# Two transformer blocks on one core: key scores searched in on-chip memory while queries are formed, a new order of the side work, and an earlier handover to the down weights

## The reference, cut to what matters

```
q = (ht @ peer_wq).reshape(T, 8, 256)                      # T = 512 tokens, 8 heads
s1 = einsum("thd,hnd->thn", q[..., :128], k1)              # 128 keys per half
s2 = einsum("thd,hnd->thn", q[..., 128:], k2)
v1, i1 = top_k(s1, 16);  v2, i2 = top_k(s2, 16)
cand = v1[..., :, None] + v2[..., None, :]                 # 16 x 16 pairs
sc, pos = top_k(cand, 16)
experts = i1[pos // 16] * 128 + i2[pos % 16]               # 128 of 16384 a token
gates = softmax(sc)
a = gelu(peer_u[experts] . h) * gates
out = sum over the 128 experts of a * peer_v[experts]
```

## Time and profile before

| | |
|---|---|
| median of 3 runs | 3027.76 us (3025.11 to 3029.04) |
| the profiled execution's own time | 3026.6 us |
| its span, first to last instruction | 3024.8 us |
| mean granted TensorE clock | 0.973 |
| busy share of the span: PE, DVE, ACT, POOL | 94%, 74%, 49%, 20% |
| moved between memory and chip | 746.30 MB, 247 GB/s on average |

### The profile page before, as it was taken

The page is one execution under the profiler, slowest core; times in us unless marked ns, Lnnn a source line. Parts: engine busy times, 40 slices in busy tenths (PEclk is TensorE's granted clock), DMA queues, the critical chain, the costliest instruction groups (busy, mean ns, idle before and its releaser), DMA issues.

```text
span 3024.8 us, 37310 instructions
## 1 busy us (share of the span) xinstructions
PE 2845.1 (94%) x13639; PEld 2369.9 (78%) x13639; DVE 2236.1 (74%) x3019; ACT 1481.4 (49%) x1990; POOL 598.8 (20%) x480
## 2 busy tenths in 40 slices
PE   5979987999999989999999998898999999999998
PEld 3657756888888758776777788898999987888887
DVE  6465547888888853797954329999997867888886
ACT  3443235878888733544452432564665633333332
POOL 0200111111111100000000010033234434444442
PEclk7999988999999999999999998999999999999999
DMA  7544535999999833232333334587789999999995
GB/s 300 169 159 157 198 132 219 362 371 366 362 354 356 305 130 114 96 119 84 105 132 132 129 119 157 180 306 264 273 303 361 337 373 341 365 367 360 362 362 187
DMA packets 203628, 746.30 MB, mean 247 GB/s; under 512 B 24752, under 2 KB 78128, under 8 KB 146352
## 3 DMA queue, kind: packets, MB, share of 16 engines
q1 hardware_dynamic: 124656, 497.12, 45.8%
q0 software_dynamic: 56912, 179.26, 16.9%
q10 hardware_dynamic: 21872, 67.48, 5.8%
HBM read 670.80 MB, written 98.11 MB: 254 GB/s over the span
## 4 chain that ended last, share of the span: by engine, by line
PE 56%; DVE 18%; issue 5%; ACT 3%; DMA 3%; ACTq 0%; DVEq 0%; POOL 0%; SPq 0%; POOLq 0%
PE PS L550 48%; DVE wlo L1897 3%; DVE oh L2673 2%; DVE hf L2687 2%; DVE hf L2699 1%; PE PS L1151 1%; ACT whi L1227 1%; PE PS L1017 1%; PE PS L1029 1%; PE PS L856 1%; ACT HH L1867 1%; DVE zo L2422 1%; DVE sS L2726 1%; DVE i L2569 1%; DVE wkk L2572 1%
## 5 line engine op out<-in xcount | busy, mean ns | idle before, releaser
L1897 DVE TENSOR_TENSOR wlo<-raw,whi 128x2048 fp32r<-128x2048 f32 x392 | 894.7, 2289 | 351.8 <-ACT whi L1227 313.9
L1227 ACT ACTIVATE whi<-raw 128x2048 fp32r<-128x2048 f32 x392 | 750.9, 1916 | 361.2 <-PE PS L550 305.3
L550 PE MATMUL PS<-HH,whi 128*128 128x512 f32 (+1 forms) x2056 | 792.0, 385 | 47.8 <-DVE wlo L1897 24.0
L550 PE MATMUL PS<-HH,wlo 128*128 128x512 f32 (+1 forms) x2056 | 754.6, 367 | 0.0
L550 PE MATMUL PS<-HL,whi 128*128 128x512 f32 (+1 forms) x2056 | 753.3, 366 | 0.0
L550 PEld LDWEIGHTS PS<-HH,whi 128*128 128x128 f32 x2056 | 392.7, 191 | 108.6 <-DVE wlo L1897 25.4
L550 PEld LDWEIGHTS PS<-HL,whi 128*128 128x128 f32 x2056 | 392.9, 191 | 46.3 <-issue 7.7
L550 PEld LDWEIGHTS PS<-HH,wlo 128*128 128x128 f32 x2056 | 391.8, 191 | 43.1
L550 PE MATMUL PS<-whi,HH 128*128 128x512 f32 (+1 forms) x896 | 352.9, 394 | 15.9 <-DVE HL L2729 10.6
L550 PE MATMUL PS<-whi,HL 128*128 128x512 f32 (+1 forms) x896 | 348.2, 389 | 0.0
L550 PE MATMUL PS<-wlo,HH 128*128 128x512 f32 (+1 forms) x896 | 348.1, 389 | 0.0
(11 more groups left out here) (436 smaller groups left out, 3903.4 us busy)
## 6 DMA issues: line engine op xcount, KB each, us to landing
raw<-in_moe_dram SPq DMA_DIRECT2D x192, 1024.0 KB, 7.4
raw<-in_u_units_dram SPq DMA_DIRECT2D x64, 1024.0 KB
raw<-in_v_units_dram SPq DMA_DIRECT2D x64, 1024.0 KB
raw<-in_w_in_dram SPq DMA_DIRECT2D x44, 1024.0 KB
raw<-in_w_ada_dram SPq DMA_DIRECT2D x24, 1024.0 KB, 22.4
acts_dram<-sS ACTq DMA_DIRECT2D x64, 384.0 KB
gates_dram<-XT ACTq DMA_DIRECT2D x24, 1024.0 KB
sS<-acts_dram SPq DMA_DIRECT2D x42, 384.0 KB
```

Source lines behind the costliest of these rows:

```text
L550: ins = t.matmul(dst, a, b, start=(first and n == 0), stop=(last and n == 2))
L1227: a.inc(a.e.activation(m.whi[p % HRING][:, :, :], m.raw[RAW_SLOT[load_of(p)]][:, :, :], ACT.Copy), "hi", p)
L1897: v.inc(v.e.tensor_tensor(m.wlo[h][:, :, :], m.raw[RAW_SLOT[load_of(p)]][:, :, :], m.whi[h][:, :, :].bitcast(F32), ALU.subtract), "lo_v", p)
```

## The change

It has four parts. (1) Scores: ACT copies them to a pair of buffers, and DVE searches each block right there (`found`, 16 calls for four token tiles each), between its weight splits in the query stage; the store, the loads and `sN` are gone, and results for all tiles are kept. (2) The order of side work: 10 choice steps a tile in place of 13, the picking cut in four, a DVE that is planned to start 13 us late, at most 2 us ahead of PE's plan in place of 4, 120 rows in the up stage in place of 116, an even pace, and earlier ends of the gates and rows. The gate work that ended at n = 120 ends at n = 116, rows that ended at 126 end at 121. (3) The handover: the gated activations of unit 0 are formed during step 127, in columns 0 to 127, and PE's first down unit starts with token tile 3, whose banks are free, and waits for each bank's gelu by itself. (4) SP loads activations of unit 0 ahead of the gates, and small tiles move in memory.

```diff
-CHOICE_NS = (4900,) * 4 + (1500, 4600, 0, 4600, 0, 8200, 6900, 800, 700)
+CHOICE_NS = (1500, 4600, 4600, 2000, 3400, 3400, 3400, 3400, 800, 700)
-LAST_GATE, LAST_ROW, UP_ROWS = 121, 126, 116
+FOUND_NS = 13000
+LAST_GATE, LAST_ROW, UP_ROWS = 117, 121, 120
...
-    tensor, vector = 0, 0
+    tensor, vector = 0, FOUND_NS
...
-        if len(chosen) < NT:
-            row_from, row_count, pace = n, c, 0.75 * (0 in chosen)
-        else:
-            pace = (UP_ROWS - row_count) / (LAST_ROW - row_from)
-        while 0 in chosen and c - row_count < pace * (n - row_from + (len(chosen) < NT)) and c < UP_ROWS:
+        rows = chosen.get(0, n)
+        while 0 in chosen and c * (LAST_ROW - rows) < UP_ROWS * (n - rows) and c < UP_ROWS:
...
-        while a < CHOICE_STEPS * NT and vector < tensor + 4000:
+        while a < CHOICE_STEPS * NT and vector < tensor + 2000:
...
+FIRST_TILES = (3, 1, 2)
+def first_slot(ci, i):
+    return (NT - TD // 128) * ci + i - TD // 128
+def gated_halves(m, u):
+    if u == 0:
+        return [x[:, 0:2 * NT - 2 * (TD // 128), 0:TD] for x in (m.HH, m.HL)], m.sA[0][:, :, :].rearrange(
+            "p c (i t) -> p (c i) t", t=TD)
+    k = u % 4
+    return [x[:, 2 * k:2 * k + 2, TD:] for x in (m.HH, m.HL)], m.sA[u % 3][:, :, :]
... pe_peer, down
-            for i in range(TD // 128, NT):
+            for i in (FIRST_TILES if u == 0 and ci == 0 else range(TD // 128, NT)):
...
-                        pe.wait_ge("act", 127)
-                        pe.wait_ge("gput", N_GATE - 1)
+                        if bank < 4:
+                            pe.wait_ge("act", 124 + bank)
+                        else:
+                            pe.wait_ge("gput", N_GATE - 1)
... act_scores
-        if k:
-            a.wait_ge("score_out", k - 1)
-        a.inc(s.activation(m.sc[:, :, :].rearrange("p t n -> p (t n)"), m.PS[:, k % 4, :], ACT.Copy), "sscore", k)
+        if k > 1:
+            a.wait_ge("found", k - 2)
+        a.inc(s.activation(m.sc[:, k % 2, :, :].rearrange("p t n -> p (t n)"), m.PS[:, k % 4, :], ACT.Copy),
+              "sscore", k)
...
+    act_high(a, m, FIRST["u_units"] + HRING - 1)
     score(15)
     a.mark("scored")
-    a.wait_all("scored")
-    a.wait_ge("score_out", 15)
... act_peer
+        if n == 127:
+            prepare(0)
         for step in PEER[n][0]:
... dve_scores
-    for n in range(8):
-        dve_low(v, m, FIRST["wq"] + n + HRING - 1)
+    def found(k):
+        v.wait_ge("sscore", k)
+        dve_top16(v, [(m.v16[:, i, k, :], m.i16[:, i, k, :], m.sc[:, k % 2, i, :], m.wkk[:, i, :]) for i in range(NT)])
+        v.also("found", k)
+    for n in range(4):
+        if n:
+            found(4 * n - 2)
+            found(4 * n - 1)
+        dve_low(v, m, FIRST["wq"] + 2 * n + HRING - 1)
+        dve_low(v, m, FIRST["wq"] + 2 * n + HRING)
+        found(4 * n)
+        found(4 * n + 1)
+    found(14)
+    dve_low(v, m, FIRST["u_units"] + HRING - 1)
+    found(15)
... dve_choice_step
-    if r < 4:
-        v.wait_ge("scores_in", i)
-        dve_top16(v, [(m.v16[:, k, :], m.i16[:, k, :], m.sN[:, k, :], m.wkk[:, k - 4 * r, :])
-                      for k in range(4 * r, 4 * r + 4)])
+    if r == 0:
+        if step == 0:
+            v.wait_all("scored")
... dve_peer
     for n in range(128):
+        if n == 127:
+            v.wait_all("open")
+            v.wait_ge(f"gate5_out{(N_GATE // 4 - 1) % 2}", N_GATE // 4 - 1)
+            v.wait_ge(f"gate5_out{N_GATE // 4 % 2}", N_GATE // 4 - 2)
+            gate_acts(0)
...
-    prepare(0)
+    low_acts(0)
... pool_scores
-    for k in range(16):
-        g.wait_ge("sscore", k)
-        g.dma(e.dma_start(bass.AP(m.sd, 128 * k, [[2048, 128], [128 * 2048, 4], [1, 128]]), m.sc[:, :, :]),
-              "score_out", k)
... sync_program
     y.wait_all("open")
+    acts(0)
     y.wait_ge(f"gate5_out{(N_GATE // 4 - 1) % 2}", N_GATE // 4 - 1)
     y.wait_ge(f"gate5_out{N_GATE // 4 % 2}", N_GATE // 4 - 2)
     gates(0)
-    acts(0)
```

More of the change, by code:

```diff
@@ L337, in __init__ @@
         self.mod = sb(ctx, "mod", [128, 48])
-        self.epst = sb(ctx, "epst", [128, 1])
-        self.eps2 = sb(ctx, "eps2", [128, 1])
-        self.warm = sb(ctx, "warm", [128, 1])
+        few = sb(ctx, "few", [128, 8])
+        self.epst, self.eps2, self.warm, self.ss = (few[:, a:b] for a, b in ((0, 1), (1, 2), (2, 3), (4, 8)))
         self.fn = sb(ctx, "fn", [128, 8])
@@ L514, in __init__ @@
                 self.paf = sb(s2, "paf", [128, 8, 16])
-                self.io16 = sb(s2, "io16", [128, 16])
+                self.some = sb(s2, "some", [128, 32])
+                self.io16, self.gs = self.some[:, 0:16], self.some[:, 16:24]
                 self.gt = sb(s2, "gt", [128, NT, 8, 16])
@@ L1847, in activation, with prepare @@
                   f"act_out{u % 2}", u)
+    def prepare(u):
+        (high, _), src = gated_halves(m, u)
+        a.wait_ge("gated", u)
+        if u:
+            a.wait_ge(*(("down", u - 4) if u >= 4 else ("up", 127)))
+        a.inc(s.activation(high, src, ACT.Copy), "ahi", u)
     for n in range(128):
@@ L2627, in dve_choice_step @@
+                                  bass.AP(m.v16, 256 * i + 16, [[1024, 128], [32, 8], [0, n], [1, width]]), ALU.add), "pick")
+    elif r in (1, 2):
+        h = 4 * (r - 1)
         pairs = [bass.AP(m.cand, N_PAIR * k, [[1024, 128], [1, N_PAIR]]) for k in range(h, h + 4)]
         dve_top16(v, [(m.sc16[:, k, :], m.pos[:, k, :], pairs[k - h], pairs[k - h]) for k in range(h, h + 4)])
-    elif r in (9, 10):
-        which = r - 9
-        if which == 0:
-            dve_pair_ranks(v, m)
-        picked = (bass.AP(m.paf, 0, [[128, 128], [1, 64], [0, 16]]), bass.AP(m.wkk, 384, [[512, 128], [1, 64], [0, 16]]),
-                  bass.AP(m.paf, 64, [[128, 128], [1, 64], [0, 16]]), bass.AP(m.wkk, 448, [[512, 128], [1, 64], [0, 16]]))
-        v.wait_ge("const5", "io16")
-        for half in range(2):
-            v.own()
-            v.inc(e.tensor_tensor(m.EQF, picked[2 * half + which],
-                                  bass.AP(m.io16, 0, [[16, 128], [0, 64], [1, 16]]), ALU.is_equal), "pick")
-            v.own()
-            v.inc(e.tensor_tensor(m.EQ, m.EQ, bass.AP(m.i16f, 128 * half + 16 * which,
-                                                      [[256, 128], [32, 4], [0, 16], [1, 16]]), ALU.mult), "pick")
-            v.own()
-            v.inc(e.tensor_reduce((m.e1, m.e2)[which][:, i, 4 * half:4 * half + 4, :], m.EQ, AX.X, ALU.add), "pick")
-    elif r == 11:
@@ new lines, in dve_choice_step @@
+    elif r == 3:
+        dve_pair_ranks(v, m, i)
+    elif r in (4, 5, 6, 7):
+        which, half = divmod(r - 4, 2)
+        ranks = bass.AP(m.wkk, 384 + 64 * half, [[512, 128], [1, 64], [0, 16]]) if which else bass.AP(
+            m.paf, 64 * half, [[128, 128], [1, 64], [0, 16]])
+        v.wait_ge("const5", "io16")
+        v.own()
+        v.inc(e.tensor_tensor(m.EQF, ranks, bass.AP(m.some, 0, [[32, 128], [0, 64], [1, 16]]), ALU.is_equal), "pick")
+        v.own()
+        v.inc(e.tensor_tensor(m.EQ, m.EQ, bass.AP(m.i16f, 128 * half + 16 * which,
+                                                  [[256, 128], [32, 4], [0, 16], [1, 16]]), ALU.mult), "pick")
+        v.own()
+        v.inc(e.tensor_reduce((m.e1, m.e2)[which][:, i, 4 * half:4 * half + 4, :], m.EQ, AX.X, ALU.add), "pick")
+    elif r == 8:
@@ L2659, in dve_choice_step @@
         v.own()
-        v.inc(e.tensor_tensor(G3, G3, bass.AP(m.gs, 0, [[8, 128], [1, 8], [0, 16]]), ALU.mult), "gt", i)
+        v.inc(e.tensor_tensor(G3, G3, bass.AP(m.some, 16, [[32, 128], [1, 8], [0, 16]]), ALU.mult), "gt", i)
 def dve_gate_step(v, m, step):
@@ L3034, in pool_peer @@
     for n in range(128):
-        for step in PEER[n][0]:
-            i, r = choice_of(step)
-            if step == 0 or r == 4 and step + CHOICE_STEPS < NT * CHOICE_STEPS:
-                if step:
-                    g.wait_ge("sn_free", i)
-                    i = choice_of(step + CHOICE_STEPS)[0]
-                g.dma(e.dma_start(m.sN[:, :, :].rearrange("p k n -> p (k n)"),
-                                  m.sd[128 * i:128 * i + 128, :, :].rearrange("t k n -> t (k n)")), "scores_in", i)
         for step in PEER[n][2]:
```

91 lines of the change are left out of this document (37 added, 54 removed).

## The result

| | before | after |
|---|---|---|
| median | 3026.44 us (3023.00 to 3029.04, 4 runs) | 2983.92 us (2980.53 to 2989.07, 4 runs) |
| ratio, 95% interval | | 0.9862 [0.9843, 0.9881] |
| profiled execution: own time, span | 3026.6, 3024.8 us | 2980.53, 2978.8 us |
| mean granted clock | 0.973 | 0.979 |

When both kernels ran again on one chip, the difference was 38.5 us (3022.87 and 2984.37).

A forecast was written before the change was run, and what follows sets the result against it. The up stage was taken as bound by a late DVE at a few places, not by PE as a whole. 3026.6 - 22.4 (up stage) - 4.7 (handover) - 2.4 (down stage) = 2997, median 2998 us; range 2985 to 3010.

The forecast's parts named there:

- The start of the sum: Whole kernel: start from the profiled execution's 3026.6 us, with the median of the runs 1.2 us above that execution.
- The down stage: Down stage: 136 rows instead of 140 bring 0, since DVE isn't its bound; less traffic for a late row brings 2.4 us.
- the late row: Early down stage: a row at 2516.79 held a split; PE waited 3.1 us, clock cost 1.7; half taken as saved, 2.4 us.
- The up stage: Up stage: bound by a late DVE at a few places; 50 us of loss become 26, net 22.4 us saved.
- Exp waits behind steps 21, 39 and 58: Up stage, tiles 0, 2 and 3: PE waits 7.6, 6.5 and 10.2 us for Exps that wait for DVE.
- The searches: Query stage: searches of 5.2 us, 84 us in all, leave the up stage; DVE full, PE not delayed, cost nothing.
- the slower rival: Query stage: searches taking 8 us hold up PE, losing 39 us against 29.5 saved, 3037; chance 0.04.
- the likeliest rival: Start of the down stage: unit 1's activations come as late as before, PE waits 3.5 us, 3003; chance 0.25.
- my 4.7: Handover from up to down stage: 3.0 us of PE idle and 1.7 us of slow clock saved.
- The rival of the clock: Up stage: slowed matmuls cost 0.37 us per idle one, so 26 us of waits cost 9.6, not 1.7: 3006; chance 0.08.
- My case against the rule in the prediction: Up stage: charging half of throttled time makes 20 us, where the row leaves room for 13.4, so it reads too much.
- DVE is never late again: Up and down stages: three Exp waits and half the down stage's go too, 2970; needs DVE's list 8% shorter; chance 0.07.

The follow-up runs named there:

- the repeat of before: The unchanged kernel before, run and profiled once more: 3022.40 us, ratio 1.0001.
- the new order with 140 rows: Changed kernel with 116 rows in the up stage instead of 120, still ended by step 121, so 140 rows in the down stage: 2984.14 us, ratio 0.9873.
- the repeat of the changed kernel: The changed kernel, unaltered, run and profiled again: 2984.37 us, ratio 0.9868.
- The added MAX8: Changed kernel with one more MAX8 pass of four in each of the 16 searches: 2996.46 us, ratio 0.9911.
- the old order with all else new: Changed kernel with the old pace of rows and choices (rows until step 126, 116 in the up stage), 10 choice steps kept: 3006.36 us, ratio 0.9939.
- the moves alone: Kernel before with only the small tiles moved in memory as in the change: 3016.85 us, ratio 0.9981.
- the searches alone: Changed kernel with the old order and old handover, keeping 10 choice steps and the moves of small tiles: 3006.36 us, ratio 0.9933.
- the version without the new handover: Changed kernel with unit 0 prepared behind step 127 again and the old order of tiles, bank waits and first loads: 2986.72 us, ratio 0.9875.
- with an even pace: Changed kernel with each Exp moved later on ACT, two steps behind its inputs, and no 2 us lead for choice steps: 2960.86 us, ratio 0.9796.

## Why the prediction was right or wrong

The forecast was 2998; the runs gave 2983.92 and 2984.37. The sign was right, the size 14 us short. Its parts:

1. **The start of the sum (4.9 us).** "3026.6 (this execution's own time", with 1.2 added for a median of 3027.76. The kernel before has medians of 3022.0 to 3023.8 in the four later sets of runs. The profile that I had read was one of its slower executions, by the 6.1 us ahead of the query stage. It was no fault of the sum, but the range had no term for it.
2. **The down stage (5.7 us): the step that failed.** "136 rows instead of 140 in it: DVE isn't its bound, 0", and "I take half, 2.4 us" for the late row. The forecast took 4.1 us off this stage (the clock behind the handover among them); it lost 9.8 (531.9 to 522.1). The late row is the larger error. In the repeat of before, PE waits 3.57 us at unit 6. 6.8 us at half clock lie around the end of that wait, 5.8 of them with PE at work (a matmul every 0.43 us in place of 0.23), which loses 2.7. That makes 6.3 us (4.6 in the first profile, by the same reading), and all of it went where half of 4.8 was booked. The rows were no zero either. DVE is indeed not the stage's bound, busy for 424 of 522 us, but PE follows `HL`. Rows per unit go by whole numbers: 140 rows make 16 units with three, 136 make 12, and a wait of some 0.2 us stands two units behind nearly each of these (units 9, 13, 17, ... before; 7, 12, 17, ... after). Behind the handover there are 16 waits before and 12 after. These small ones are worth 1 us in all; more comes from the one long wait, since every profile with 140 rows (six) has one of 1.7 to 3.6 us in the down stage, at unit 6 or 49, and none of the eight with 136 has one over 0.6. Four rows were worth 3.3 us on the changed kernel and 7.9 on the kernel before; the new order with 140 rows 6.5. The two overlap, since either alone removes the wait at unit 6. Why that one gather is late stays open.
3. **The up stage (1.5 us).** Together with the gap behind it 26.9 us went, 25.4 were forecast (22.4 and 3.0). The mechanism was the one named: DVE ahead of the first split, no `wlo` waits, Exp waits behind steps 21, 39 and 58. In its terms three errors nearly cancel. The floor is 620.0, not 623. The waits are 1.1, 9.1, 4.0 and 5.5, where 2, 7.6, 6.5 and 10.2 were worked out: 19.7 for 26.3. And slowed matmuls cost 647.8 - 620.0 - 19.7 = 8.1 us, where I had 1.7. I had reasoned that "slowed matmuls behind the first waits cost nothing where DVE sets the time". That held for the sum (27.8 above the measured floor, 28.0 above the worked-out one forecast) and not for its parts: a slowed PE comes later to the next Exp and waits less. That the sums agree to 0.2 us is luck.
4. **Stages ahead (1.4 us)**, costed at nothing: 1670.4 us from the first matmul to the query stage in the repeat of before, 1669.0 after. It can't be told from scatter, since the repeat of the changed kernel has 1671.7. The moves of small tiles are measured at 6 us by the runs; that this is their addresses was not shown.

These make 13.5 of the 14.1 us.

**The searches.** "25.6 us of work in 25.4, so it is full, but late by 0.2 us a group only", and "I cost this at nothing": the cost is right, PE's stage stays at 103.3 us. DVE is a little later than that: a search takes 5.24 us where a split follows, as below, and 5.42 from one to the next, and its groups follow each other in 26.1 us (25.6 worked out):

```profile
1744.40 0.88 DVE L2595 MAX8 v<-sc 128x8 f32<-128x128 f32 x4
...
1749.64 4.47 DVE L1913 TENSOR_TENSOR wlo<-raw,whi 128x2048 fp32r<-128x2048 f32 x2
```

DVE was forecast at over 95 us of the stage and has 92.5. The added MAX8 tests the slower rival's sum: 0.9 us more for a search make 3.6 us a group, and three and a half groups 13 us; 12.1 were measured. By that rate 7.4 us for a search would cost 29 us, so its point was well placed. That PE would be held up in the query stage at all came already at 6.1 us.

**The handover.** The gap went as forecast (from the last up start to the first down start 3.33 us before, 0.18 after), and unit 1, the likeliest rival, waits 0.5 us. What it is worth may hang on the order: 2.3 to 3.1 us with the new one, between 0 (medians) and 2.4 (stages of the profiles) with the old, all of it within the scatter of medians. The 1.7 us of clock in my 4.7 are there in some profiles of before and not in others.

**The rival of the clock** had 0.37 us of slowed matmuls for each idle one; the trace after has 8.1 for 19.7, or 0.41, so as a rate it was the better guess. The Trainium skill ("TensorE: Matmul & The Clock Gate", the section on HAM oscillation) charges half of all throttled time; the up stage after has slow stretches of 10.2, 3.4 and 6.8 us, which would make 10.2, and the row leaves 8.1. Here the rule is near, and over by the part that passes while PE is idle: that is 5.3 of the 20.4 us, and half of the rest is 7.6. My case against the rule in the prediction came from rounded figures. The up stage of its profile has 34.1 us of slow stretches, which make 17 by the rule and not 20, and with the measured floor of 620.0 the row leaves 16.4 and not 13.4.

**The late DVE.** "DVE is never late again" was given 0.07, at 2970, because "It needs DVE's list 8% shorter than I add it up". It doesn't: moving one wait on ACT gives 2956 with DVE's work unchanged. The same missing idea, that the Exp's place in ACT's queue is a free choice, is behind the 26 us of waits that the prediction took as given.

## What to carry to other kernels

When a wait of one engine stands in a queue in front of work that the bound engine needs, count what is behind it before counting how long the producer takes: three steps of distance between DVE's last operation and ACT's Exp took off 28 us, while 60 us of DVE work moved elsewhere took off 10.5. Then look at the next operation in that queue: with an even pace the Exp was on time and the compares were late. In a stage where an engine has 20% to spare, the pieces per period still matter by whole numbers, and a term of zero for them should be bounded by the longest wait that they can start. Profile the kernel before twice before a sum goes by one execution: 8.4 us of 3025 lay between two executions here, 6.1 of it ahead of the change.

## What the runs showed of the hardware

The same gap of PE, 2.9 us at the 5774th matmul (1405 to 1411 us), is followed by a stretch at the half clock of 3.4 or 6.8 us in five of the fourteen profiles, and by none in nine. The stage around it takes 341.2 to 342.3 us in the five and 339.1 to 339.3 in the nine. So an idle time of that length may cost nothing beyond itself or 2 to 3 us more. Both kernels that were profiled twice did the same both times, and an edit far from this stage goes with a change of it: the old order with all else new has 6.8 us at half clock there, the changed kernel none. Whether the edit causes it or chance does isn't shown. The handover's gap of 3.0 us has 3.4 us of half clock at it in the first profile of before, with the moves alone and with the searches alone, and none in the repeat of before or in the version without the new handover.
